# Four tiles step by step over k, with their weights in that order, at the head of every stage behind a norm

## What is computed

```python
def hybrid_layer(h, p_i, pos, lb, norm_g, w_in, w_out, ffn1_gu, ffn1_down, ...):
    h = h + 0.5 * rmsnorm_2(swiglu(rmsnorm_2(h, norm_g[0]), ffn1_gu, ffn1_down), norm_g[1])
    z = rmsnorm_2(h, norm_g[2]) @ w_in
    ...
    mixed = jnp.concatenate([o_a, o_b, o_c], axis=-1) @ w_out
    h = h + rmsnorm_2(mixed, norm_g[3])
    h = h + 0.5 * rmsnorm_2(swiglu(rmsnorm_2(h, norm_g[4]), ffn2_gu, ffn2_down), norm_g[5])
    gate = jax.nn.sigmoid(rmsnorm_2(h, norm_g[6]) @ ple_gate)
    h = h + rmsnorm_2((p_i @ ple_proj) * gate, norm_g[7])
```

## Time and profile before

| | |
|---|---|
| Time, median of 3 runs | 2953.34 us (2951.21 to 2958.8) |
| The profiled execution: its own time | 2953.6 us |
| its span | 2951.8 us |
| granted TensorE clock, mean over the span | 0.966 |
| TensorE matmul busy | 2743.0 us (93%) |
| ScalarE, VectorE, GpSimd busy | 36%, 47%, 37% |
| High casts (L433) and low splits (L376), mean | 1059 ns and 2426 ns, 396 of each |

### The profile page before, as it was taken

How to read it: one execution, slowest core, us unless ns; L and a number is a source line. 1 busy time by engine, 2 the same in 40 slices (tenths; PEclk the granted TensorE clock), 3 DMA queues, 4 the chain that set the end, 5 groups by cost and what they waited for, 6 DMA issues and landing times. The chain is left out here.

```text
span 2951.8 us, 31821 instructions
## 1 busy us (share of the span) xinstructions
PE 2743.0 (93%) x12038; PEld 2091.2 (71%) x12038; DVE 1394.5 (47%) x1803; ACT 1063.1 (36%) x1598; POOL 1086.6 (37%) x472
## 2 busy tenths in 40 slices
PE   8899797988999999888999999999998978999997
PEld 2788563325788887766788887788886846888875
DVE  0888307996244303756534204644216674544115
ACT  2323224654333223344432324432324344333233
POOL 0223224654354443321444443344443212444432
PEclk9999899999999999998999999999999989999999
DMA  7212120003233332210233333233332101233331
GB/s 262 72 58 79 50 86 0 0 1 104 68 110 100 93 100 70 79 50 26 82 100 94 99 95 91 79 100 94 99 97 73 58 29 57 87 99 95 98 100 50
DMA packets 63333, 235.11 MB, mean 80 GB/s; under 512 B 7265, under 2 KB 7521, under 8 KB 62689
## 3 DMA queue, kind: packets, MB, share of 16 engines
q1 hardware_dynamic: 61056, 222.33, 24.0%
q10 hardware_dynamic: 2144, 10.92, 1.0%
HBM read 231.12 MB, written 2.10 MB: 79 GB/s over the span
## 5 line engine op out<-in xcount | busy, mean ns | idle before, releaser
L376 POOL TENSOR_TENSOR wlo<-raw,whi 128x1024 fp32r<-128x1024 f32 x396 | 959.5, 2426 | 1692.7 <-ACT whi L433 1692.7
L1491 PE MATMUL banks<-xhi,whi 128*128 128x512 f32 x2016 | 802.2, 398 | 31.3 <-ACT xhi L455 30.1
L433 ACT ACTIVATE whi<-raw 128x1024 fp32r<-128x1024 f32 x396 | 418.0, 1059 | 1078.9 <-PE banks L1500 901.2
L1492 PE MATMUL banks<-xhi,wlo 128*128 128x512 f32 x2016 | 792.7, 393 | 0.0
L1500 PE MATMUL banks<-xlo,whi 128*128 128x512 f32 x2016 | 768.4, 392 | 0.3 <-DVE xlo L1244 0.3
L1491 PEld LDWEIGHTS banks<-xhi,whi 128*128 128x128 f32 x2016 | 383.2, 190 | 123.3 <-issue 40.8
L1492 PEld LDWEIGHTS banks<-xhi,wlo 128*128 128x128 f32 x2016 | 383.8, 190 | 82.3 <-issue 3.1
L1500 PEld LDWEIGHTS banks<-xlo,whi 128*128 128x128 f32 x2016 | 382.2, 190 | 81.4 <-DVE xlo L1244 0.8
L874 DVE TENSOR_TENSOR sq_sum<-sq_sum,tmp 128x512 f32<-128x512 f32 x102 | 113.1, 1108 | 424.0 <-ACT tmp L448 424.0
L1491 PE MATMUL banks<-act_hi,whi 128*128 128x512 f32 x704 | 273.9, 389 | 0.0
L1492 PE MATMUL banks<-act_hi,wlo 128*128 128x512 f32 x704 | 273.9, 389 | 0.0
(11 more groups left out here) (326 smaller groups left out, 3142.9 us busy)
## 6 DMA issues: line engine op xcount, KB each, us to landing
raw<-in_stream SPq DMA_DIRECT2D x420, 512.0 KB, 3.5
h<-in_x ACTq DMA_DIRECT2D x2, 2048.0 KB, 11.1
dft_t<-in_dft_t ACTq DMA_DIRECT2D x1, 2048.0 KB, 8.8
out<-h SPq DMA_DIRECT2D x4, 512.0 KB, 2.6
ctx_raw<-in_ctx ACTq DMA_DIRECT2D x1, 1024.0 KB, 17.6
ple_raw<-in_ple ACTq DMA_DIRECT2D x2, 512.0 KB, 3.8
mixpar<-in_mixpar ACTq DMA_DIRECT2D x2, 384.0 KB, 3.6
table<-in_table ACTq DMA_DIRECT2D x1, 577.0 KB, 6.7
```

Of the source, the lines that this page charges most:

```text
L376: pool.tensor_tensor(wlo[:, i], raw[:, i], whi[:, i].bitcast(F32), ALU.subtract)\
L433: act.activation(whi[:, u % SLOTS], raw[:, u % SLOTS], ACT.Copy)\
L1491: pe.matmul(acc[acc_of[t]][:], whi[:, u % SLOTS, i], x_h, start=(k == 0), stop=False)
L1492: pe.matmul(acc[acc_of[t]][:], wlo[:, u % SLOTS, i], x_h, start=False, stop=False)
```

## The change

In the eight stages behind a norm, four tiles instead of three and a half go together over k. Their 32 blocks now lie in the stream in the order of k (step 0 of tiles 0 to 3, step 1 of tiles 0 to 3, and so on), so a unit holds two steps of four tiles. `place` gives the unit and position of a block, and `leads_first` reorders the arrays. `sum_squares` (`after_first`) now stands inside the last step: behind its eight high-part matmuls and ahead of its four low-part ones.

```diff
-                side = 3 if side_by_side else 1
-                order = []
-                for k in range(k_tiles):
-                    order.append(([*range(side)], k))
-                    if side_by_side and k % 2:
-                        order.append(([side], k // 2))
-                group_end = len(order)
-                order += [([side], k) for k in range(k_tiles // 2 if side_by_side else 0, k_tiles)]
-                order += [([m], k) for m in range(side + 1, tiles) for k in range(k_tiles)]
-                for n, (ms, k) in enumerate(order):
+                leads = LEADS if leading else 1
+                order = [([*range(leads)], k) for k in range(k_tiles)]
+                order += [([m], k) for m in range(leads, tiles) for k in range(k_tiles)]
+                for ms, k in order:
...
-                        if k == 0 and t >= 4:
+                        if k == 0 and earlier[t] is not None:
 
                             pe.wait_ge(*(bank_free(earlier[t]) or (ev.sem("product"), 1)))
-                        b = first_block[stage] + m * k_tiles + k
-                        u, i = b // UNIT, b % UNIT
+                        u, i = place(stage, m, k, k_tiles, leads)
...
+                    if leading and m < leads and k == k_tiles - 1:
+                        after_first()
                     for m in ms:
...
-                    if n + 1 == group_end and after_first:
-                        after_first()
-                    if k == k_tiles - 1 and ms[0] >= side and after_tile:
-                        after_tile(ms[0])
+                    if k == k_tiles - 1 and (m >= leads or not leading):
+                        if after_tile:
+                            after_tile(m)
+
+            def place(stage, m, k, k_tiles, leads):
+
+                b = first_block[stage] + (k * leads + m if m < leads else m * k_tiles + k)
+                return b // UNIT, b % UNIT
...
+def leads_first(blocks):
+
+    n = LEADS * KT
+    first = blocks[:n].reshape(LEADS, KT, P, P).transpose(1, 0, 2, 3).reshape(n, P, P)
+    return np.concatenate([first, blocks[n:]])
```

More of the change, by code:

```diff
@@ L35 @@
 SLOTS = 4
+LEADS = 4
 UNIT = 8
@@ L1464, in _, with product @@
         def _(pe):
-            def product(stage, tiles, k_tiles, hi, lo, source, key, after_first=None, side_by_side=False, after_tile=None):
-                side = 3 if side_by_side else 1
-                order = []
-                for k in range(k_tiles):
-                    order.append(([*range(side)], k))
-                    if side_by_side and k % 2:
-                        order.append(([side], k // 2))
-                group_end = len(order)
-                order += [([side], k) for k in range(k_tiles // 2 if side_by_side else 0, k_tiles)]
-                order += [([m], k) for m in range(side + 1, tiles) for k in range(k_tiles)]
-                for n, (ms, k) in enumerate(order):
+            def product(stage, tiles, k_tiles, hi, lo, source, key, after_first=None, leading=False, after_tile=None):
+                leads = LEADS if leading else 1
+                order = [([*range(leads)], k) for k in range(k_tiles)]
+                order += [([m], k) for m in range(leads, tiles) for k in range(k_tiles)]
+                for ms, k in order:
                     x_h, x_l = (hi[:, k], lo[:, k]) if hi is not None else (mix1_hi(k), mix1_lo(k))
@@ L1898, in lay_out_second @@
             gu = blocks_of(i[f"ffn{s + 1}_gate_up_2"][l]).reshape(2, FT, KT, P, P)
-            weights.append(gu.transpose(1, 0, 2, 3, 4).reshape(-1, P, P))
+            weights.append(leads_first(gu.transpose(1, 0, 2, 3, 4).reshape(-1, P, P)))
             weights.append(blocks_of(i[f"ffn{s + 1}_down_2"][l]))
             if s == 0:
-                weights.append(blocks_of(i["w_in_2"][l][:, order]))
+                weights.append(leads_first(blocks_of(i["w_in_2"][l][:, order])))
                 weights.append(blocks_of(i["w_out_2"][l][order_out]))
-        weights.append(blocks_of(i["ple_gate_2"][l]))
+        weights.append(leads_first(blocks_of(i["ple_gate_2"][l])))
         weights.append(blocks_of(i["ple_proj_2"][l]))
```

## The result

| | median us | lowest to highest | runs |
|---|---|---|---|
| before | 2953.27 | 2951.21 to 2958.8 | 6 |
| changed | 2965.98 | 2964.9 to 2970.89 | 6 |

The changed kernel takes 1.0045 times the time of before, with a 95% interval of 1.0033 to 1.0058: 13 us more, between 10 and 17. Its profiled execution took 2969.69 us with a span of 2967.9. So that execution is 16.1 us longer than the profiled one of before (span 2951.8), and 3.7 us above its own median.

A forecast was written before the change was run, and what follows sets the result against it. The prediction took TensorE as the bound of the whole stage head. Its terms, 9.2 us for six stages and 3.6 for two "in2" stages, made 12.8 us: 2966.4 for the profiled execution, 2966.0 for the median, range 2957 to 2975.

The forecast's parts named there:

- the "in2" term: Two "in2" stages: reads and tile 4 already hang on the sum, so its whole 1.81 us goes through twice, 3.6 us.
- What bounds the head: Stage heads behind a norm: TensorE is the bound throughout; fuller k steps have no wait to win, 0 us.
- The square sum 1.81 us later, and 4.1 us from it to tile 4: Stage heads: the sum stands behind 92 matmuls instead of 84, 1.81 us later; tile 4 follows it by 4.1 us.
- Six stages, 1.53 us each, 9.2 in all: "gu" and "gate" heads: tile 4 waits for its bank, 1.42 us plus 0.11 for a slower first matmul, 9.2 us together.
- Weights in the order of k, and GpSimd's earlier split: 0: Stage heads: unit 4 is cast 2.44 us earlier and its split runs beside VectorE's clears in "in2"; no time effect, 0.
- The clock in the new idles: Tile 4's new idles: no clock loss in six stages (1.26 us); in "in2" (3.0, 1.8) any loss precedes long recurrence waits.
- the second rival: The clock falls in each new gap before tile 4, costing 7.5 to 18 us more, 2973.5 to 2984 us; chance 10%.
- Part of it is given back: Rival: both "in2" stages give back all 3.6 us, plus one VectorE collision of 2 us, 2960.4 us; chance 14%.
- The clock falls in each gap: Rival: TensorE's clock drops in six new gaps before tile 4, 1.25 to 3.05 us each, 2973.5 to 2984; chance 10%.
- VectorE's collisions go away: Rival, "in2": eight slowed VectorE instructions, 14.6 us together, dissolve as GpSimd's unit 4 moves away, giving 2951.4 us; chance 3%.
- No effect: Rival: tile 4 isn't waiting for the bank, so the sum's place costs nothing and time stays at 2953; chance 2%.

The follow-up runs named there:

- e3: The kernel before with only the weights of the first four tiles laid out in the order TensorE takes them: 2954.29 us, ratio 1.0001.
- e2: The kernel before with only its square sum eight matmuls later, four matmuls ahead of tile 4: 2966.03 us, ratio 1.0039.
- e1: The changed kernel with the square sum moved back ahead of the last k step, behind 84 matmuls: 2957.08 us, ratio 1.0006.
- e4: The changed kernel with the tiles of "gu" and "gate" rotating over seven PSUM banks instead of four: 2963.17 us, ratio 1.0023.
- e9: The changed kernel with seven banks in "gu" and "gate" and one more weight cast ahead of 1/rms in "gate": 2957.35 us, ratio 1.0008.
- e5: The changed kernel with the square sum behind all 96 matmuls of the first four tiles instead of 92: 2977.03 us, ratio 1.0081.
- e8: The changed kernel with the square sum ahead of step 6, and steps 6 and 7 taken tile by tile: 2946.28 us, ratio 0.9976.
- e10: The changed kernel with the square sum ahead of step 6 everywhere, and steps 6 and 7 tile by tile in "in2" alone: 2949.28 us, ratio 0.9986.
- e7: The changed kernel with the square sum ahead of step 6, behind 72 matmuls, tiles still step by step: 2957.73 us, ratio 1.0014.

## Why the prediction was right, point by point

The forecast was 2966.0 us, and the median is 2965.98. That close a hit is luck: the interval of the ratio is 0.25% wide, some 7 us, and in the profile the "in2" term came out near its size by errors of opposite sign, as told below. (The terms as they stand add up to 2966.1.)

**What bounds the head.** Right. TensorE had no idle in the k loop before, and has none after. e3 shows that the order of the weights alone is no term.

**The square sum 1.81 us later, and 4.1 us from it to tile 4.** Right. The sum is behind 92 matmuls, and it is followed by tile 4 after 4.10 us in the seventh head. The place alone, set into the kernel of before (e2), gives the loss back in full, and taken out of the change (e1) removes nearly all of it.

**Six stages, 1.53 us each, 9.2 in all.** Right in mechanism and about right in size. The six idles are 1.29 us for the 1.26 predicted, the first matmul after them lasts 0.50 us as predicted, and the "gu" and "gate" stretches grew by 5.9 + 3.4 = 9.3 us in the change's profile, by 7.6 + 3.6 = 11.2 in e2's. The spread between the two is the half-clock stretch at each head, which the prediction had named as what the range must hold. Where that stretch is the same, at the first "gu" head of before and of e2, the stage grew from 369.36 to 370.92 us: 1.56 us. One sentence was too strong, though: that no later wait in the stage could take a part of it. e4 shows one, the split of unit 5 in "gate". It is covered while tile 4 waits, and costs 1.3 us twice as soon as tile 4 doesn't. The total of the change is not touched by it.

**Two "in2" stages, 1.81 us each, 3.6 in all.** Right as far as the reads, and not what the stages then cost. The waits for `z`, 3.03 and 1.83 us, are as predicted, and the two stretches together have 4.4 us more, but not twice 1.81: layer 0 went from 269.3 to 274.4 us, layer 1 from 272.9 to 272.3. In e2, e4 and e9, with the same two waits, layer 0 has 271.3, 270.9 and 271.0, and layer 1 has 272.4, 273.3 and 272.4.

The step that failed is that TensorE's own delay there doesn't count and that the 1.81 us reach the end of the stage as they are. The chain did move by about that much: counted from the head's first high part, the first matmul behind the wait for `hg_att` starts in layer 1 at 56.9 us instead of 55.2, in the change and in e2 alike. In layer 0 it starts at 56.6 (the change) and 55.6 (e2) instead of 53.7. What came behind it was the clock. The first 15 us behind that wait, before in layers 0 and 1, then changed in layers 0 and 1 (windows, columns as above; idle before them 6.71, 8.01, 4.42 and 6.42 us):

```profile
1207.94:1222.94 15.00, 15.00 (x95) 0.84 0.11 36
2285.00:2300.00 15.00, 14.99 (x83) 0.67 0.11 36
...
1213.20:1228.20 15.00, 14.97 (x81) 0.67 0.13 36
2300.70:2315.70 15.00, 15.00 (x96) 0.85 0.13 35
```

That is 2.5 us more lost in layer 0, and 2.7 us given back in layer 1. In layer 0 there were two more terms that the sum didn't have: ScalarE's cast, waiting for the slow tile 4, held the recurrence's chain for 2.7 us, and a collision of 2.1 us on `diff` (2.78 us before, 0.69 now) was gone. All of these are as large as the term itself and have both signs. So the 3.6 us are not shown, and that the stretches came near them is luck. Why the clock behind the same idle stays low for longer in one profile than in another is open.

**Weights in the order of k, and GpSimd's earlier split: 0.** Right (e3). Unit 4 is cast right behind ScalarE's k loop, and its split is over before the square sum.

**The clock in the new idles.** Right for the six: 1.00 behind each. In e5 the idles grew to 2.22 us, and two of six were followed by 0.59 and 0.71. So the second rival's mechanism exists, but not at the idles that the change makes in "gu" and "gate". By the rows of "gu" and "gate" a gap of 1.29 us costs its own length; by those of "in2" a longer one can cost some 3 us more (6.10 us at 0.50 behind 3.03). The Trainium skill (page "TensorE: Matmul & The Clock Gate", section "Part 1: The HAM clock gate") asks to avoid idle gaps only above a length that is greater than 1.29 and than 1.83 us; the prediction cites it without that limit. For the six the rows agree with it; for the 1.83 us of idle in "in2", with 0.71 behind it, they don't.

**The rivals.** "Part of it is given back" didn't show in the time, but its mechanism is there: in the change's profile layer 1 gave its delay back and a collision in layer 0 was gone, while layer 0's longer half clock took as much; in e2, e4 and e9 the "in2" stretches are longer by 1.2 to 2.0 us only. "The clock falls in each gap" would have shown 0.5 in six windows and didn't; it fell in the two of "in2". "VectorE's collisions go away" is nearly as it was forecast: one of eight went, six stayed, and one in layer 1 moved from `gate_b` (2.67 us before) to `q_dec` (2.88 us). That no reordering of four tiles removes them was too strong: in e8 and e10 five are left. "No effect" is excluded by e1 and e2.

## What to carry to other kernels

Where a reduction's result gates the release of accumulators, find for each group of tiles the two events that the first read needs, the result and the closing of the first tile, and put both ahead of the group's end by the length of the read's chain; moving only one of them stops at the other (e7), moving both won 0.24% here (e8). Taking all the tiles of a group in step closes them all at the end, and that costs even when the data is on time: keep the last steps tile by tile. And when a wait is removed, look for the next one that it covered (the split behind the bank in "gate"), since a part of the gain may stay there.

## What the runs showed of the hardware that I had not expected

*The clock behind an idle of TensorE is not a function of its length alone.* In these kernels: behind 1.29 us 1.00 in all six heads of the change; behind 1.83 us 0.71 in the change and 1.00 in e4; behind 2.22 us 1.00 four times, 0.59 and 0.71; behind 3.03 us 0.50 in the change; behind 3.96 us 0.67 (e5, 1189.21 to 1192.70). Two rows of e4, both in "in2", behind 3.0 and 1.83 us:

```profile
1188.70:1192.20 3.50, 3.50 (x9) 0.58 0.37 101
2266.95:2270.40 3.45, 3.45 (x15) 1.00 0.27 64
```

*A stage with the same waits can differ by 3 us between profiles.* The seven head-to-head stretches of e3 agree with before to 0.05 us, but two kernels with the same waits at tile 4 (the change and e2) differ by 3.1 us in the "in2" stage of layer 0, where the lower clock lasted longer behind two idles, 3.03 and 4.42 us. A single profile therefore doesn't decide about a term of 2 us; two kernels that are alike in that stage, or a comparison of several runs, are needed.
